# Nine small parameter loads issued from ScalarE's queue instead of SP's

## The reference

```python
cond_act = jax.nn.silu(cond)                       # c for latent tokens, c_ctx for context tokens
for layer in range(2):
    shift, scale, gate = split(cond_act @ w_mod[layer] + b_mod[layer], 3)
    hm = rmsnorm(x, norm_g[layer]) * (1 + scale) + shift
    out = fc_mixer(hm, ...) if layer == 0 else ssd_mixer(hm, ...)   # Fourier and short conv; bidirectional SSD scan
    x = x + gate * out
return rmsnorm(x, final_norm_g), states
```

## Time and profile before

| | |
|---|---|
| median of three runs | 1255.61 us (1254.97 to 1257.90) |
| span of the profiled execution, first to last instruction | 1252.9 us |
| mean granted TensorE clock | 0.982 |
| TensorE busy | 1166.6 us, 93% of the span |
| VectorE, ScalarE, POOL busy | 797.4, 451.8, 280.3 us |
| DMA | 148.04 MB, mean 118 GB/s |

### The profile page before, as it was taken

One profiled execution on the slowest core, in us unless ns is written; L12 is line 12 of the kernel. 1 busy time (PEld: TensorE's weight loads), 2 busy tenths in 40 slices (PEclk: granted clock), 3 DMA queues, 4 the chain that ended last, 5 costly groups with the idle time before them and its releaser, 6 DMA issues. The chain is left out here.

```text
span 1252.9 us, 19236 instructions
## 1 busy us (share of the span) xinstructions
PE 1166.6 (93%) x7179; PEld 1048.0 (84%) x7179; DVE 797.4 (64%) x1372; ACT 451.8 (36%) x830; POOL 280.3 (22%) x421
## 2 busy tenths in 40 slices
PE   6799999999999999997988989998999898979995
PEld 1389888899999998886888988998899898957884
DVE  1553344175858433647669797879797979777525
ACT  3321222122212123335444535454545454445222
POOL 1110000000000000002105353545354544454001
PEclk9999999999999999998999999999999999989998
DMA  8551223144444325223224342425252525272802
GB/s 335 165 168 36 83 84 94 41 135 134 144 126 151 99 70 202 79 68 134 60 74 124 91 128 80 144 68 155 69 156 68 155 68 156 67 257 74 296 6 84
DMA packets 175674, 148.04 MB, mean 118 GB/s; under 512 B 6796, under 2 KB 156724, under 8 KB 175220
## 3 DMA queue, kind: packets, MB, share of 16 engines
q1 hardware_dynamic: 170996, 130.22, 33.5%
q0 software_dynamic: 4608, 16.83, 4.1%
HBM read 134.25 MB, written 12.78 MB: 117 GB/s over the span
## 5 line engine op out<-in xcount | busy, mean ns | idle before, releaser
L259 DVE TENSOR_TENSOR w_lo<-raw_w,w_hi 128x1024 fp32r<-128x1024 f32 x128 | 157.0, 1229 | 87.0 <-ACT w_hi L253 84.7
L288 PE MATMUL PS<-h_hi,w_hi 128*128 128x320 f32 x768 | 177.1, 312 | 6.5 <-DVE h_lo L362 5.5
L288 PE MATMUL PS<-h_lo,w_hi 128*128 128x320 f32 x768 | 175.5, 310 | 0.0
L288 PE MATMUL PS<-h_hi,w_lo 128*128 128x320 f32 x768 | 175.2, 309 | 0.0
L253 ACT ACTIVATE w_hi<-raw_w 128x1024 fp32r<-128x1024 f32 x128 | 134.2, 1051 | 111.0 <-PE PS L288 77.2
L1113 PE MATMUL PS<-h_hi,w_hi 128*128 128x320 f32 x512 | 127.3, 330 | 17.7 <-DVE big L1302 7.1
L288 PEld LDWEIGHTS PS<-h_hi,w_hi 128*128 128x128 f32 x768 | 128.3, 188 | 11.5 <-issue 5.8
L288 PEld LDWEIGHTS PS<-h_lo,w_hi 128*128 128x128 f32 x768 | 129.0, 188 | 0.0
L288 PEld LDWEIGHTS PS<-h_hi,w_lo 128*128 128x128 f32 x768 | 128.8, 188 | 0.0
L1113 PE MATMUL PS<-h_hi,w_lo 128*128 128x320 f32 x512 | 119.4, 315 | 0.0
L1113 PE MATMUL PS<-h_lo,w_hi 128*128 128x320 f32 x512 | 118.7, 314 | 0.0
(11 more groups left out here) (203 smaller groups left out, 2152.1 us busy)
## 6 DMA issues: line engine op xcount, KB each, us to landing
raw_w<-in_fc_w_in_dram SPq DMA_DIRECT2D x48, 512.0 KB, 4.2
raw_w<-in_ssd_w_in_dram SPq DMA_DIRECT2D x48, 512.0 KB, 5.2
big<-l_scr SPq DMA_DIRECT2D x40, 512.0 KB, 4.2
big<-in_w_mod_dram POOLq DMA_DIRECT2D x16, 1024.0 KB, 5.4
raw_w<-in_fc_w_out_dram SPq DMA_DIRECT2D x16, 512.0 KB, 3.3
raw_w<-in_ssd_w_out_dram SPq DMA_DIRECT2D x16, 512.0 KB, 7.7
big<-in_w_mod_dram SPq DMA_DIRECT2D x6, 1024.0 KB, 18.0
y_scr<-big SPq DMA_DIRECT2D x40, 128.0 KB, 1.8
```

What stands on the lines that cost most here:

```text
L259: dve.tensor_tensor(w_lo[:, slot, :], raw_w[:, slot, :], w_hi[:, slot, :].bitcast(F32), ALU.subtract).then_inc(lo_ready, 1)
L288: mm = pe.matmul(PS[:, 2 * pair + s, 0:HALF], w[:, slot, ws], h[:, kt, s * HALF:(s + 1) * HALF], start=(kt == 0 and n == 0), stop=(kt == K ...
```

## The change

The nine small loads leave SP's program and stand, in the same order and on the same semaphores, at the head of ScalarE's program.

```diff
@@ -1490,15 +1490,6 @@
         @block.sync
         def _(sp):
 
-            sp.dma_start(cond[:, 0, :], A["c"].rearrange("a (p t) -> (a p) t", t=KT)).then_inc(cond_landed, 16)
-            sp.dma_start(cond[:, 1, :], A["c_ctx"].rearrange("(p t) -> p t", t=KT)).then_inc(cond_landed, 16)
-            sp.dma_start(cst[:, :], A["consts"]).then_inc(par_landed, 16)
-            sp.dma_start(praw[0:96, 0, :], A["ssd_conv_w"].rearrange("a k (t n) -> (a k t) n", n=P)).then_inc(par_landed, 16)
-            sp.dma_start(praw[96:128, 0, :], A["ssd_conv_b"].rearrange("a (t n) -> (a t) n", n=P)).then_inc(par_landed, 16)
-            sp.dma_start(praw[0:16, 1, :], A["norm_g"].rearrange("a (t n) -> (a t) n", n=P)).then_inc(par_landed, 16)
-            sp.dma_start(praw[16:40, 1, :], A["fc_conv_w"].rearrange("a k (t n) -> (a k t) n", n=P)).then_inc(par_landed, 16)
-            sp.dma_start(praw[40:56, 1, :], A["ssd_norm_g"].rearrange("a (t n) -> (a t) n", n=P)).then_inc(par_landed, 16)
-            sp.dma_start(praw[56:72, 1, :], A["b_mod"].rearrange("a (t n) -> (a t) n", n=P)[0:16, :]).then_inc(par_landed, 16)
             xs = A["x_sample"][0].rearrange("(t p) d -> p t d", p=P)
             for s in range(8):
                 if s == 7:
@@ -1614,6 +1605,15 @@
 
         @block.scalar
         def _(act):
+            act.dma_start(cond[:, 0, :], A["c"].rearrange("a (p t) -> (a p) t", t=KT)).then_inc(cond_landed, 16)
+            act.dma_start(cond[:, 1, :], A["c_ctx"].rearrange("(p t) -> p t", t=KT)).then_inc(cond_landed, 16)
+            act.dma_start(cst[:, :], A["consts"]).then_inc(par_landed, 16)
+            act.dma_start(praw[0:96, 0, :], A["ssd_conv_w"].rearrange("a k (t n) -> (a k t) n", n=P)).then_inc(par_landed, 16)
+            act.dma_start(praw[96:128, 0, :], A["ssd_conv_b"].rearrange("a (t n) -> (a t) n", n=P)).then_inc(par_landed, 16)
+            act.dma_start(praw[0:16, 1, :], A["norm_g"].rearrange("a (t n) -> (a t) n", n=P)).then_inc(par_landed, 16)
+            act.dma_start(praw[16:40, 1, :], A["fc_conv_w"].rearrange("a k (t n) -> (a k t) n", n=P)).then_inc(par_landed, 16)
+            act.dma_start(praw[40:56, 1, :], A["ssd_norm_g"].rearrange("a (t n) -> (a t) n", n=P)).then_inc(par_landed, 16)
+            act.dma_start(praw[56:72, 1, :], A["b_mod"].rearrange("a (t n) -> (a t) n", n=P)[0:16, :]).then_inc(par_landed, 16)
             act.wait_ge(cond_landed, 32)
             act.activation(cond[:, :, :], cond[:, :, :], ACT.Silu).then_inc(cond_ready, 1)
             norm_act(act, 0, xn, xT0)
```

## The result

In paired runs the kernel after took 1259.44 us (median of 20), the kernel before 1255.35 us (20). The ratio of after to before is 1.0029, 95% interval 1.0018 to 1.0039: slower by 3.6 us, between 2.3 and 4.9. The forecast was 1253.5, 2.15 us faster, in a range from 1251.4 to 1257.5. (The time around the span, taken as 2.7 us before, is 1.8 in the profiled execution of the kernel after, 1259.24 less 1257.4; the argument does not hang on it.)

The account below looks back on a forecast made before the run. DMAs were taken to bound the start up to 20.25 us, then TensorE. Small loads landing at 8.0 put the first product at 8.65 and s = 2 at 18.1, gaining 2.15 us: 1253.5, range 1251.4 to 1257.5.

Parts of the forecast that it names:

- I take 8.0: Start of the kernel: the last small load lands at 8.0 us instead of 6.13, at 1.55 small packets per large one.
- one small for one large: Bound on the last small load's landing: small and large packets alternate at the shared engines, so it lands at 10.5 us.
- nothing passes: Rival: small loads take turns one for one, or the mixer's start gives the gain back; 1255.6 to 1255.9 us, chance 0.12.
- Slower, by starvation: Rival at the DMA engines: two large packets served per small one, last landing 17.5, loss 7.3, 1262.9 us; chance 0.05.
- the prediction's own sign of being wrong: At TensorE's wait for the small loads: the prediction is wrong if L549 starts after 10.2 us.
- general formula: At TensorE's first product: the gain is 10.85 us less the product's start, up to a limit of 2.81 us.
- about 1 us in either direction: TensorE's clock, in the first turn and the mixer's first matmuls, may move things by about 1 us either way.
- Long turns: Rival: an engine takes 16 large packets, 2.5 us, before changing queue; nine such waits, loss 15, about 1270; chance 0.03.
- the cap: Limit at TensorE's turn s = 2: gain 2.81 us, 4.09 at best; as rival 1252.8 to 1251.5, chance 0.25.
- Blocked issue: Rival: SP's full queue blocks ScalarE's issues too, last small load lands at 15.8, loss 5.6, 1261.2 us; chance 0.05.
- no gap from wm[7]: wm[7] waits for TensorE's first turn, about 2 us late; loads landing 17 us after issue leave no gap.
- the three slower ones: Rivals that are slower: starved small packets 1262.9 us, long queue turns about 1270, blocked issues 1261.2; chances 0.05, 0.03, 0.05.

Follow-up runs that it names:

- e10: The kernel after, unchanged, run again in the same rounds as a kernel with five extra small loads; ratio to the kernel before 1.0030 (1.0018 to 1.0042).
- e5: The kernel after with wm[0] brought by two loads of 512 KB instead of one of 1 MB; one run, L549 at 11.52 us, mixer 2.60 us late.
- e3: The kernel after with five of the nine small loads back on SP, ahead of the large loads, four on ScalarE; ratio to the kernel before 0.9998.
- e4: The kernel before with nine more 4 KB loads on SP's queue between small and large loads; ratio to the kernel before 1.0039 (1.0024 to 1.0055).
- e9: The kernel before with five more 4 KB loads on SP's queue ahead of the large loads; ratio to the kernel before 1.0021 (1.0010 to 1.0032).
- e11: The kernel before with wm[0] issued first, ahead of the nine small loads, all on SP's queue; ratio to the kernel before 0.9980 (0.9968 to 0.9992).
- e7: The kernel after with c, c_ctx and cst back on SP, the other six small loads on ScalarE; ratio to the kernel before 0.9998 (0.9982 to 1.0014).

## Why the prediction was wrong

The step that failed is the term "I take 8.0", the landing of the last small load. It set the rate at which small packets get through by the one row where two queues met, 134 beside 208 packets, 1.55 small for one large. That row is of POOL's queue carrying the large packets and SP's the small ones. Between ScalarE's queue and SP's it is 578 beside 600, 0.96 for one. The bound named "one small for one large" was thus near the rate, and it gave 10.5; the measured 11.77 (12.16 in e10, 11.52 in e5) is 1.0 to 1.7 above it. It left out the pause: from 2.5 to 5.0 us ScalarE's queue stood almost still, 16 packets beside 228, which `c` before it and `c_ctx` behind it, passing fast, only in part made up for. Its 44 packets for each engine are 45 (724 in all, for the earlier trace rows end before the last had landed). The pitch of ScalarE's issues is off too, by 0.54 to 0.455, but they were all out by 5.5 us and did not decide.

The mechanism is then that of the rival "nothing passes", turns of one for one, which had 0.12 and gave 1255.9; it had the loss too small. "Slower, by starvation" (0.05) had the point from which it decides, 10.2, which is also the prediction's own sign of being wrong, but two large packets for each small one is not what the queues did. The general formula, start of the first product less 10.85, gives 12.29 - 10.85 = 1.44, and the first turn, slower than the plan's, took the other 0.9 (18.04 - 12.29 = 5.75 against 4.85). 1.44 + 0.9 makes the measured 2.35. The prediction had allowed about 1 us in either direction for such turns, and this is that microsecond. In e10 the turn was as quick as before, and there the formula alone is right: 12.69 - 10.85 = 1.84, measured 1.82. (By the prediction's own terms the 10.85 should be 20.25 - 9.46 = 10.79; nothing hangs on the difference.)

Why the turn took longer the MATMULs of L557 show. The kernel after from 12.2 to 16.9 us and from 18 to 21.5, then the kernel before from 10 to 12.9 (count: least/median/most ns of one, first and last start):

```profile
L557 PE MATMUL PS<-big,cond x6: 835/1061/1062, 12.3 to 16.5; 128*2 128x512 f32 x6
...
L557 PE MATMUL PS<-raw_w,cond x8: 592/592/593, 18.0 to 21.0; 128*2 128x512 f32 x8
...
L557 PE MATMUL PS<-big,cond x4: 767/1034/1057, 10.1 to 12.6; 128*2 128x512 f32 x4
```

The first ones start every 0.84 us and the later ones every 0.43, so they run at half pace, which is the lower of the clock's two levels (1.2 GHz); before, four run so, in the kernel after six. The clock column reads 1.00 there all the same, but it has no reading behind it: the trace's clock records begin with 1.00 at 12.9 us before and at 17.0 after (15.5 in e10), just where the half pace ends, and the column prints 1.00 where there is no record. What the turn takes beyond 3.60 is about half of the time from its start to that record: 2.31 beside 4.70 / 2 after, 1.39 beside 2.84 / 2 in e10, and so in every profile. TensorE had done nothing but the two transposes before the turn in each of them, and how long the low level lasted, 2.7 (e3) to 5.7 us (e5), does not follow the change.

"Long turns" appeared in part. The Trainium skill, "DMA: Bandwidth & Descriptors", section "Queues, rings and completion order", has an engine drain a whole packet, typically 9 to 17 descriptors, before it turns to the next queue. The pause between 2.5 and 4.5 us in the kernel after (177 packets beside 14) looks like one such turn, of wm[0]'s 16, and the 142 packets behind it like the answering turn of `c_ctx`'s 9. That happened once in the kernel after, where the rival had it nine times, and the one for one from 5.5 to 10.5 us does not agree with turns of that length. The Trainium skill's section "Issuing engines are not separate DMA queues" of the same page, by which alone the prediction's sum would have been the cap, says that transfers from several engines interleave and that only issue time is saved. The trace agrees (404 packets between 434, and 4.09 us of SP's issues saved), but the section does not say what interleaving costs the small load that is waited for, which decided here. "Blocked issue" did not happen: ScalarE's issues took at most 0.74.

Right were: SP's start at 0.74; the table load behind the issues and hidden; the tokens landing earlier by roughly the 2.8 us of the plan (3.4); wm[0] not waited for; no gap from wm[7]; and that a shift at the product reaches the end (e4). The forecast's sign was lost because it rested on a gain that depended on one unmeasured rate, with bounds of 6.13 and 10.5 around a break-even of 10.2. The upper bound stood beyond the break-even and still got only 0.25 of the chance (nothing passes 0.12 and the three slower ones 0.13).

The profiled span grew by 4.5 us, 2.1 more than the mixer's lateness. The shift of VectorE's instructions between the two profiles is 2.35 us up to 560 us and then jumps where TensorE's granted clock falls to 0.50 in one and not in the other: 2.6 at 655 us, 4.2 at 700. The windows of 655 to 700 us, kernel after and kernel before (last three columns clock, DMA share, GB/s):

```profile
655.00:700.00 45.00, 41.51 (x275) 40.16 (x273) 42.03 (x87) 21.47 (x47) 20.59 (x30) 0.96 0.38 109
```

```profile
655.00:700.00 45.00, 41.49 (x290) 40.15 (x289) 44.10 (x96) 22.52 (x50) 22.70 (x33) 1.00 0.38 109
```

The same loss at this place (0.96) stands in e9's profile, which has no load on ScalarE's queue, and in e11's, which is faster; only the kernel before, e3 and e4 have 1.00 there. So it is not the change's doing. Whether a shift of the start makes such falls likelier stays open.

## What to carry to other kernels

Moving small loads to another engine's queue saves issue time and gives up their place in front of the large ones: at the shared engines each small packet, semaphore writes included, then waits for about one large one. Count packets for each engine, not bytes (45 here, in 0.3 MB), before splitting queues, and if the work behind the small loads is first on the path, leave them ahead or put a single large load before them on the same queue. Where a bound of an unmeasured rate lies beyond the break-even, give that side its full chance.

## What the runs showed that was not expected

Two hardware queues alternate packet by packet whatever the sizes: in 5 us of the kernel after 434 of SP's, of 4 KB, beside 404 of ScalarE's, of 512 and 1536 bytes, the 4-byte semaphore writes of both counted; in 2 us of e5 187 beside 167, nearly all of 32 bytes. The exceptions are pauses of about 2 us in which one queue gets next to nothing (177 beside 14; in e7 195 beside 1). A load of 4 KB that landed in 1.9 us from SP's queue in the kernel before took 4.8 us beside a 1 MB load. Issues on ScalarE came at a pitch of 0.54 us while SP issued too, and of 0.48 when it did not. TensorE's first turn of eight MATMULs took from 4.92 to 6.42 us in the profiles of this study, for the same work, since it began at the lower clock level each time and stayed there for 2.7 to 5.7 us; that spread is as large as most of the gains that were sought.
